# Stick-breaking mixer: the stays in two fp32r halves, two fp32r products in place of one plain fp32 product

## What is computed

```python
z = einsum('bhqd,bhkd->bhqk', qb, kb) * scale
causal = kpos[None, :] < qpos[:, None]
log_stay = where(causal, log_sigmoid(-z), 0.0)
log_after = cumsum(log_stay, axis=3, reverse=True) - log_stay
weights = where(causal, exp(log_sigmoid(z) + log_after), 0.0)
outs.append(einsum('bhqk,bhkd->bhqd', weights, vb))
```

## Time and profile before

| | |
|---|---|
| median of 3 runs | 2876.05 us (2847.34, 2876.05, 2877.9) |
| profiled execution, own time | 2885.94 us |
| its span | 2884.1 us, so 1.84 us lie outside |
| mean granted TensorE clock | 0.963 |
| TensorE busy | 2603.6 us (90%) |
| VectorE busy | 2058.0 us (71%) |
| ScalarE busy | 1275.5 us (44%) |
| the stick-breaking stretch | 277.5 to 315.6 us of the span |

### The profile page before, as it was taken

How to read it: one execution, slowest core, us unless ns; L and a number is a source line. 1 busy time by engine, 2 the same in 40 slices (tenths; PEclk the granted TensorE clock), 3 DMA queues, 4 the chain that set the end, 5 groups by cost and what they waited for, 6 DMA issues and landing times.

```text
span 2884.1 us, 38765 instructions
## 1 busy us (share of the span) xinstructions
PE 2603.6 (90%) x12692; PEld 2019.4 (70%) x12692; DVE 2058.0 (71%) x4105; ACT 1275.5 (44%) x2145; POOL 1138.0 (39%) x1481
## 2 busy tenths in 40 slices
PE   8998999999999978889899989999896888887777
PEld 7887788788788866778798978788775433333322
DVE  7886588788688754667687856676685777767775
ACT  5555555655555554344354545445452222222221
POOL 4434145254244310457556733333001444444443
PEclk9999999999999998789899999999998999999999
DMA  9986799699699872334354689999756999999998
GB/s 357 372 307 243 270 392 373 227 395 373 223 357 379 275 250 99 102 121 152 122 179 150 188 320 386 372 385 384 252 199 229 409 421 421 412 417 420 416 421 336
DMA packets 217832, 873.30 MB, mean 303 GB/s; under 512 B 38320, under 2 KB 38448, under 8 KB 184048
## 3 DMA queue, kind: packets, MB, share of 16 engines
q0 software_dynamic: 118496, 511.47, 45.4%
q1 hardware_dynamic: 99072, 359.38, 34.8%
q10 hardware_dynamic: 144, 1.05, 0.1%
HBM read 786.70 MB, written 152.17 MB: 326 GB/s over the span
## 4 chain that ended last, share of the span: by engine, by line
PE 64%; DMA 18%; DVE 9%; issue 4%; ACT 3%; POOL 1%; another core or an unknown queue 0%; SPq 0%; DVEq 0%; POOLq 0%; ACTq 0%
PE ps L1738 13%; PE ps L1739 13%; PE ps L1740 12%; DMA arena<-both_rows,arena 12%; PE ps L1812 11%; PE ps L2154 6%; PE ps L1814 6%; DMA both_rows<-in_stream 5%; DVE arena L1635 2%; DVE w_lo L1057 1%; PE ps L2120 1%; DMA raw<-in_stream 1%; PE ps L1913 1%; ACT w_hi L639 1%; PE ps L1784 1%
## 5 line engine op out<-in xcount | busy, mean ns | idle before, releaser
L1057 DVE TENSOR_TENSOR w_lo<-raw,w_hi 128x1024 fp32r<-128x1024 f32 x665 | 811.0, 1223 | 379.6 <-ACT w_hi L639 296.9
L639 ACT ACTIVATE w_hi<-raw 128x1024 fp32r<-128x1024 f32 x665 | 702.0, 1058 | 476.1 <-DMA raw<-in_stream 329.5
L2154 PE MATMUL ps<-arena 128*128 128x512 f32 x1024 | 479.5, 615 | 136.1 <-ACT arena L846 135.8
L1812 PE MATMUL ps<-act_both,w_hi 128*128 128x512 f32 x1408 | 502.4, 399 | 6.9 <-DVE act_both L1085 5.1
L2154 PEld LDWEIGHTS ps<-arena 128*128 128x128 f32 x1024 | 190.6, 194 | 414.2 <-ACT arena L846 218.6
L1635 DVE SCALAR_TENSOR_TENSOR arena<-arena 128x1024 f32<-128x1024 f32 x256 | 313.7, 1225 | 191.5 <-DMA arena<-both_rows,arena 189.6
L572 POOL DMA_INDIRECT arena<-both_rows,arena x256 | 295.2, 1153 | 368.1 <-PE ps L2154 333.8
L509 POOL DMA_DIRECT2D both_rows<-arena x512 | 279.2, 552 | 354.2 <-DVE arena L1134 344.4
L1738 PE MATMUL ps<-w_hi,act_both 128*128 128x512 f32 (+1 forms) x990 | 387.1, 391 | 21.4 <-DVE act_both L1708 6.1
L1814 PE MATMUL ps<-act_both,w_lo 128*128 128x256 f32 x1408 | 395.4, 281 | 0.0
L537 POOL DMA_INDIRECT gate_cells<-hot x256 | 304.2, 1188 | 215.0 <-DVE hot L1596 103.6
(11 more groups left out here) (259 smaller groups left out, 3463.9 us busy)
## 6 DMA issues: line engine op xcount, KB each, us to landing
raw<-in_stream SPq DMA_DIRECT2D x675, 512.0 KB, 3.3
arena<-in_stream POOLq DMA_DIRECT2D x128, 512.0 KB, 9.9
both_rows<-arena POOLq DMA_DIRECT2D x512, 128.0 KB, 6.3
both_rows<-in_stream POOLq DMA_DIRECT2D x128, 512.0 KB, 6.9
gate_cells<-hot POOLq DMA_DIRECT2D x32, 512.0 KB, 21.4
hot<-gate_cells POOLq DMA_DIRECT2D x128, 128.0 KB, 7.0
gate_cells<-hot POOLq DMA_INDIRECT x256
arena<-both_rows,arena POOLq DMA_INDIRECT x256, 11.0
```

The source lines that it names most:

```text
L639: act.activation(w_hi[:, u % SPLIT, :], raw[:, u % RAW, :], ACT.Copy).then_inc(hi_done, 1)
L1057: dve.tensor_tensor(w_lo[:, u % RAW, :], raw[:, u % RAW, :], w_hi[:, u % SPLIT, :].bitcast(F32), ALU.subtract).then_inc(lo_done, 1)
L1812: pe.matmul(ps[:, bank, :], high, act_both[:, :, k, :], start=k == 0, stop=k == KD - 1, skip_group_check=True)
L2154: ins = pe.matmul(ps[:, 2 * (n % 2) + half, :], diags[:, p % DIAG_RING, :], row[:, p % ROW_RING, D + 512 * half:D + 512 * half + 512], sta ...
```

## The change

The stays are written over `sizes(p)`. ScalarE then copies them to `stay_hi` in fp32r (`stays_high`), VectorE subtracts that from the stays and writes the rest to `stay_lo` in fp32r (`stays_low`), and TensorE multiplies each half with `neg_tri` and `neg_ones`, which are now fp32r too. `stay_hi` and `stay_lo` are rings of four pairs in the place of `stay`. `stay_ready`, for which `sums(p)` waits, now comes from `stays_low(p)`.

```diff
@@ ScalarE
+                def stays_high(p):
+                    act.wait_ge(stay_done, p + 1)
+                    act.activation(stays_of(stay_hi, p), sizes(p), ACT.Copy).then_inc(stay_high, 1)
+
                 softplus(0)
                 softplus(1)
+                stays_high(0)
                 weights_of(0)
                 softplus(2)
+                stays_high(1)
                 weights_of(1)
                 softplus(3)
+                stays_high(2)
                 output_high(0)
                 for p in range(2, N_PAIRS):
+                    if p + 1 < N_PAIRS:
+                        stays_high(p + 1)
                     weights_of(p)
@@ VectorE
                 def stays(p):
                     dve.wait_ge(ln_done, p + 1)
-                    dve.scalar_tensor_tensor(stay[:, 2 * p:2 * p + 2, :], logit(p), 0.0, sizes(p), ALU.max,
-                                             ALU.add).then_inc(stay_ready, 1)
+                    dve.scalar_tensor_tensor(sizes(p), logit(p), 0.0, sizes(p), ALU.max, ALU.add).then_inc(stay_done, 1)
+
+                def stays_low(p):
+                    dve.wait_ge(stay_high, p + 1)
+                    dve.tensor_tensor(stays_of(stay_lo, p), sizes(p), stays_of(stay_hi, p).bitcast(F32),
+                                      ALU.subtract).then_inc(stay_ready, 1)
@@
                 size(2)
+                stays_low(0)
                 stays(1)
                 size(3)
+                stays_low(1)
                 stays(2)
                 output_low(0)
+                stays_low(2)
                 stays(3)
                 for p in range(2, N_PAIRS):
                     if p + 2 < N_PAIRS:
                         size(p + 2)
+                    if p + 1 < N_PAIRS:
+                        stays_low(p + 1)
                     output_low(p - 1)
@@ TensorE
                 def sums(p):
                     pe.wait_ge(stay_ready, p + 1)
                     for h in range(2):
-                        z, s = logit(p)[:, h, :], stay[:, 2 * p + h, :]
-                        pe.matmul(z, neg_tri, s, start=False, stop=False, skip_group_check=True)
-                        ins = pe.matmul(z[:, P:T], neg_ones, s[:, T:PAIR], start=False, stop=True, skip_group_check=True)
+                        z = logit(p)[:, h, :]
+                        for side in (stay_hi, stay_lo):
+                            pe.matmul(z, neg_tri[:, :], stays_of(side, p)[:, h, :], start=False, stop=False,
+                                      skip_group_check=True)
+                        for side in (stay_hi, stay_lo):
+                            ins = pe.matmul(z[:, P:T], neg_ones[:, :], stays_of(side, p)[:, h, T:PAIR], start=False,
+                                            stop=side is stay_lo, skip_group_check=True)
                     ins.then_inc(c_done, 1)
```

More of the change, by code:

```diff
@@ L298, in program @@
         size_done = sem("size_done")
+        stay_done = sem("stay_done")
+        stay_high = sem("stay_high")
         stay_ready = sem("stay_ready")
@@ L372, in program @@
         keep = arena[:, :].rearrange("p (c t) -> p c t", t=T)
-        stay, logw = blk(A_STAY, HEADS, PAIR), blk(A_LOGW, HEADS, PAIR)
+        logw = blk(A_LOGW, HEADS, PAIR)
+        stay_hi = in_place("stay_hi", [P, 8, PAIR], base + 4 * A_STAY)
+        stay_lo = in_place("stay_lo", [P, 8, PAIR], base + 4 * (A_STAY + 8 * PAIR))
         sigma = tok(A_Q, D)
@@ L377, in program @@
         stick_ring = blk(A_LN, 8, PAIR)
-        neg_tri, neg_ones = area(A_TERMS, P), area(A_TERMS + P, P)
+        neg_tri = in_place("neg_tri", [P, P], base + 4 * A_TERMS)
+        neg_ones = in_place("neg_ones", [P, P], base + 4 * (A_TERMS + P))
         neg_mask = area(A_TERMS + 2 * P, P)
@@ L391, in sizes, with stays_of @@
             return stick_ring[:, 2 * (p % 4):2 * (p % 4) + 2, :]
+        def stays_of(side, p):
+            return side[:, 2 * (p % 4):2 * (p % 4) + 2, :]
         QUERY_SLOTS = RAW + SPLIT + 2
@@ L1206, in stick_terms @@
                 ahead = area(A_STICKC, P)
-                dve.tensor_scalar(neg_tri, ahead, -1.0, None, ALU.add)
+                dve.tensor_scalar(neg_tri[:, :], ahead, -1.0, None, ALU.add)
                 dve.tensor_scalar(neg_mask, ahead, -1.0, 2.0 ** 99, ALU.add, ALU.mult)
-                dve.tensor_scalar(neg_ones, area(A_STICKC + PAIR + P, P), -1.0, None, ALU.mult).then_inc(terms_ready, 1)
+                dve.tensor_scalar(neg_ones[:, :], area(A_STICKC + PAIR + P, P), -1.0, None, ALU.mult).then_inc(terms_ready, 1)
                 dve.wait_ge(terms_ready, 1)
```

## The result

Four runs of the changed kernel gave a median of 2912.21 us (2891.35 to 2924.26) against 2876.98 (2847.34 to 2882.07), a ratio of 1.0132 with an interval of 1.0078 to 1.0187. In twelve more runs of the same kernel beside 35 of the kernel before, a set of its own with other absolute times (medians 2868.58 and 2854.32), the ratio was 1.0057 (1.0013 to 1.0100), or +16 us. The profiled execution took 2903.59 us, 17.65 more than that of before.

What follows compares the result with a forecast made beforehand. The prediction took the chain of waits between VectorE and ScalarE, not TensorE, as the bound. It added +9 us from the order and +3 from the clock to the median 2876.05, giving 2888 us, range 2858 to 2903.

Steps and rivals of the forecast that it cites:

- What bounds the stretch: Stick-breaking stretch: waits between VectorE and ScalarE set 4.43 us per pair; TensorE has 0.56 us of slack.
- the rival of -7 us: TensorE was the bound after all and the additions lie in slack: -7 us, 2869; chance 0.06.
- Copy 0.83, subtraction 0.96: Per-pair ScalarE copy at 0.83 us (0.80 to 0.97) and VectorE subtraction at 0.96 us (0.92 to 1.14).
- The start (Part 4): First pairs: weights 0 and 1 and two subtractions put pairs 2 and 3 in a row; mask 4 comes 7.5 us later.
- Sums at 1.05 (Part 1): TensorE's eight fp32r products per pair take 1.05 us (0.94 to 1.18) instead of 1.93, priced by columns.
- Part 5's loop: Steady periods: a new chain through TensorE takes 4.63 us against 4.43; three periods add 0.6 us.
- The end (Part 6): Last pair: copy, subtraction and hop add about 1.8 us ahead of sums 7, themselves 0.88 shorter; total +9.0.
- The clock (Part 7): TensorE gaps over 4 us at the start bring the clock down, then it returns: about +3 us.
- the row of 1084: Profile row, 1084 to 1088: TensorE 4.00 of 4 busy with plain fp32 products, yet clock 0.50.
- The sum: Whole stretch: +9 us from the order and +3 from the clock, +12 us.
- The time: Whole kernel: 2876.05 + 12 = 2888 us against the median, range 2858 to 2903; within 1%: 0.87.
- slower by over 1%: Rival: unshortened sums at 1.2 GHz throughout, +9 + 24 + 3 = +36 us, 2912; chance 0.04.

Runs made afterwards that it cites:

- 28 fillers: Changed kernel plus unneeded small fp32r products (fillers): 28, 28 and 24 in TensorE's three start gaps, 8 behind each later mix; stretch 46.4 us.
- 48 in a row: Changed kernel plus 48 unneeded fp32r products in each of TensorE's three start gaps, none later; stretch 51.1 us, ratio 1.0049.
- 20 fillers: Changed kernel plus 20, 20 and 18 unneeded fp32r products in TensorE's three start gaps, 8 behind each later mix; stretch 50.4 us.
- the one with 36: Changed kernel plus 36, 36 and 30 unneeded fp32r products in TensorE's three start gaps, 8 behind each later mix; stretch 55.3 us, ratio 1.0029.

## Why the prediction came out as it did

- *What bounds the stretch*: right. The chain on VectorE and ScalarE sets it, TensorE had slack (short sums without the rest: the same 4.43), and the rival of -7 us fell.
- *Copy 0.83, subtraction 0.96*: measured 0.83 and 0.95.
- *The start (Part 4)*: the mechanism was right to the place: subtraction 0 where stays 1 stood, weights 0 in front of exp 2, pairs 2 and 3 in a row. Predicted +7.5 at mask 4. Measured +8.6 with the clock mostly up (28 fillers, 21.97 against 13.34), of which 0.75 are the longer sums and 0.67 the dip of the clock at sums 1, so 7.2 for the order; +11.8 in the changed kernel.
- *Sums at 1.05 (Part 1)*: this term was mis-sized. It is 1.30, outside my bounds of 0.94 to 1.18, because I priced each product by its columns and forgot what lies between unlike products. The Trainium skill's rule (TensorE: Matmul & The Clock Gate, section LDWEIGHTS), which I set aside, has 0.107 us for a weight load of 128 columns; the fillers, one new load each, came every 0.105. By that rule the sum was 1.13, still short. The 0.25 counts at sums 0, 1 and 2, in three periods and at sums 7: 7 x 0.25 = +1.8. Part 5's loop becomes 4.63 + 0.25 = 4.88; measured 4.89.
- *The end (Part 6)*: from stays 7 to the output product it took 4.99 before and 6.2 now, +1.2 against +0.9 predicted, the difference being again the sums.
- *The clock (Part 7)*: this step failed in size, and it is the larger error. That it would fall in the gaps was right. I priced the start at 1.5 to 1.6 us and one steady period at 0.8 to 1.6. Measured: sums 0 to weights 0 2.40 against 1.40, the same for pair 1, and sums 2 to mask 4 4.05 against 2.27, so 3.8 in the start (I had left out sums 2). Then two periods of 6.65 and 6.46 instead of 4.89, 3.3 more. Together 7.1, not 3. The low period itself was nearly right, 6.2 forecast, with two errors in it: sums to logits 2.39 (307.59 to 309.98) where I had 1.7, logits to mask 1.65 where I had 1.9. What was wrong is how much fell into the low spells. I expected a busy TensorE to bring the clock back; the row of 1084, which I had named against it, was the better guide.
- *The sum*: 9.0 (order, as predicted) + 1.8 + 7.1 = 17.9; measured 17.7. The stretch with 28 fillers puts the order at 11.2 - 1.8 - 0.7 (the dip) = 8.7. How much is order and how much is clock rests on that one execution.
- *The time*: 2888 was forecast and 2912 measured, above the range to 2903. By the ratio of the later and larger set, 1.0057, it is 2893 on the median of before, and the difference of the traces gives 2895. So of the 24 us missed, 6 are the two terms above. The other 18 aren't in the stretch, which no trace shows longer than 52.9; that they are the spread of four runs, in a part that the change doesn't touch, fits the larger set and the traces but isn't shown for these four, of which only one has a trace. The upper end of the range had room for the low clock but only 3 us for that spread, though the three runs known at the time were 30 us apart. That was the wrong step in the range: I widened it downward for a lucky median and not upward for an unlucky one. The rival *slower by over 1%* named 2912, which is the measured time, but by luck: its mechanism, unshortened sums at low clock throughout, didn't occur. On the larger set the ratio itself is below 1%, and its interval just reaches it.

## What to carry to other kernels

A step put in series between two engines costs by the queue that it lands in, not by its length: 1.8 us of new work per pair fitted into the idle time of both engines, and still cost some 9 us, most of it because independent work was queued behind a wait; the same instructions in another order gave 14 of 17.7 us back, the clock's share among them. Before splitting a product to make it shorter, ask if the product is on the chain, and take the price of short products of different matrices from a row with that pattern (here 1.30 us, not the 0.94 of their columns). And where a change opens gaps of several microseconds in front of TensorE, add the cost of everything after them at half clock, for as long as the nearest low stretch in the trace lasts.

## What the runs showed of the hardware

- A fp32r product of 128 columns came 0.06 us behind a like one in the sums, but 28 or 48 in a row, with a load each, came every 0.105.
- The clock stayed at 0.50 for 14 us with TensorE 90% busy, for 20 us in the run with 20 fillers, and for 23 us with 23.00 of 23 busy in the one with 36; in the rows of before it returned after 4.5 us of work. From one execution to the next of the same kernel the spells moved: the three steady periods took 6.65, 6.46 and 4.89 us in the first trace, 4.93, 4.88 and 4.89 in the second, where the clock fell at the end instead (stays 7 to the output product 7.96 us, not 6.22).
- One part of the program, about 600 us long, varies by 60 us from execution to execution with the same instructions. The granted clock goes with it (0.92 at 557 us, 0.90 at 597, 0.87 at 616). What starts it is open and wasn't tried.
